# Experts' first tile: output projection by blocks of w_out, late scores for heads 4 to 7, gathers released slot by slot

## The chip, the core and the metric

The kernel runs on one core of a Trainium2 chip. The metric is the device time of one execution in microseconds (us). One program does a whole decoder layer for 1024 new prompt tokens and 32 sample tokens (8 sequences of 4).

## What is computed

The layer is: RMS norm, one input projection, a Mamba-2 group and a differential-attention group side by side, an output projection, then a mixer of single-neuron experts (PEER), per-layer input embeddings and a final norm. The change lies where the output projection and the mixer start:

```
h = h + concat([y_ssm, y_diff]) @ w_out
m = rmsnorm(h, g_ffn)
h = h + peer(m, w_query, sub_keys, expert_u, expert_v)

def peer(xn, ...):                      # blocks of 128 tokens
    q = (xt @ w_query).reshape(blk, 8, 2, 128)
    s = einsum('thcd,cnd->thcn', q, sub_keys)
    s1, i1 = top_k(s[:, :, 0], 16);  s2, i2 = top_k(s[:, :, 1], 16)
    sc, pos = top_k(s1[..., :, None] + s2[..., None, :], 16)
    idx = i1[pos // 16] * 128 + i2[pos % 16]
    act = gelu(einsum('thkd,td->thk', expert_u[idx], xt))
    return einsum('thk,thkd->td', softmax(sc) * act, expert_v[idx])
```

Every token reads 8 heads x 16 experts = 128 rows of `expert_uv`, each 2048 float32 (8 KB).

## The kernel before, in words

The program has three stages: `project`, `attend` and `experts`. All of the change is in `experts`. Each stage is written by hand for each engine: one program for SyncE (SP), GpSimd (POOL), ScalarE (ACT), VectorE (DVE) and TensorE (PE), which meet only at semaphores. What an engine's program has earlier is done earlier, whatever is ready.

`experts` works in tiles of 128 tokens: tiles 0 to 7 are the prompt, tile 8 the sample tokens. For a tile, POOL issues 128 indirect DMAs (`ring`, line 2526), the gathers; each brings one 8 KB row of `expert_uv` for each of the 128 partitions (1.05 MB) into one of the `RING = 8` slots. The first half of a slot's row is u, the second half v. A tile is cut in four groups of 32 tokens (`rows`, the copies of the normed activations to all quarters), so that one gather serves 32 tokens with four experts each.

For each gather c, DVE multiplies u by `rows` and sums (L2644). For each pair of gathers q, ACT makes the coefficients (`gelu`, times gate, into a diagonal: L2573, L2576, L2582) and PE adds coefficient times v into `acc` (L2704: eight instructions, the V sum of the pair). The V sum raises `v_used`, and POOL waits for `v_used` before it issues the gather that takes the same slot again (gather c needs the V sum of pair (c - 8) / 2).

Between the steps of these loops every engine takes `next()` steps of generators ("sides"): the front of the next tile, and in tile 0 also what is left of the tile's own search (`rest_vector`, `rest_scalar`) and the scores of the sample rows (`few_tensor`, L1983). So a side's order among the gathers is fixed.

Tile 0's front has nothing to hide behind. `front_tensor(pe, 0)` does, in this order:

- turns the mix `m` (L1738); ACT and DVE copy it to `aT` (L1799, L1833); DVE first waits for `g_in`, the load of g_ffn
- waits for all eight blocks of `wo` (w_out, one DMA per block of 128 rows, issued by ACT at L2535), then projects into `pt[0]` and `pt[1]` (L1753): first the eight blocks for the left half, then the eight for the right
- projects the sample rows (`few_project`, L1956)
- folds `w_queryT` with the keys into `w2` (`fold_queries`, L2100), chunk by chunk, 16 chunks. The chunks are loaded into the `ring` memory by SP, in four DMAs (L2482) behind a wait for all of `wo`. Banks `pk[2]`, `pk[3]` and `acc` hold the folds; ACT and DVE copy them out (L2544, L2548, L2112)
- turns the normed `m`, scores n = 0 (heads 0 and 1) behind chunk 3, folds the other chunks, copies the rows (`copy_rows`, L2138), and scores n = 1, 2, 3 (L1783, `pk[n]`)

Only then do the loop's seed of `acc` with h1 (L2687) and the first V sum follow. In the meantime DVE searches heads 0 and 1 (`search`) and writes their indices (`first_found`, L2024, semaphore `idx0`). POOL's program begins with `fold_out(pool, 15)`, the wait for ACT's copy of the last fold, since the first gathers overwrite the memory in which w_queryT lies; then it waits for `idx0`. Slot c of the ring holds chunks 2c and 2c + 1.

Of the kernel before, what the change touches and what calls it, by code (L numbers as in the profile page):

```python
# [14 lines left out]
P = 128  # L15
D = 1024
KT = D // P
# [25 lines left out]
PH, TOPK = 8, 16  # L43
# [1547 lines left out]
def experts(nc, t):  # L1591
# [18 lines left out]
    with ExitStack() as ctx:  # L1610
        st = Stage(nc, ctx, "ex")
        wo = st.sb("wo", [P, KT, D])
        w2 = st.sb("w2", [P, KT, 2 * PH * KEYS])
# [4 lines left out]
        aT = st.sb("aT", [P, KT, P])  # L1618
# [37 lines left out]
        acc = [st.ps(f"acc{k}", [P, 512]) for k in range(2)]  # L1656
        pt = [st.ps(f"pt{k}", [P, 512]) for k in range(2)]
        pk = [st.ps(f"pk{k}", [P, 4, KEYS]) for k in range(4)]
        consts, ident_in, g_in, keys_in, wo_in = (st.sem(n) for n in ("consts", "ident_in", "g_in", "keys_in", "wo_in"))
        idx0, negated0, grown0, divided0, gates0 = (  # L1660
            st.sem(n) for n in ("idx0", "negated0", "grown0", "divided0", "gates0"))
        wq_in = [st.sem(f"wq_in{n}") for n in range(4)]
        iota_up, set_up, folded = (st.sem(n) for n in ("iota_up", "set_up", "folded"))
# [71 lines left out]
        def front_tensor(pe, k):  # L1735
            def turn():
                for c in range(KT):
                    mm = pe.transpose(pt[c // 4][:, (c % 4) * P:(c % 4 + 1) * P], m[:, c * P:(c + 1) * P], ident[:])  # L1738
                mm.then_inc(turned, 1)

            yield from pause(4)
            pe.wait_ge(x_in, 32 * (k + 1))
            turn()
            if k == 0:
                few_turn(pe, 0)
            yield from pause(8)
            pe.wait_ge(taken_a, 2 * k + 1)
            pe.wait_ge(taken_v, 2 * k + 1)
            if k == 0:
                pe.wait_ge(wo_in, 16 * KT)  # L1750
            for n in range(2):
                for c in range(KT):
                    mm = pe.matmul(pt[n][:], aT[:, c, :], wo[:, c, n * 512:(n + 1) * 512],  # L1753
                                   start=(c == 0), stop=(c == KT - 1))
                    if c == KT - 1:
                        mm.then_inc(projected, 1)
                    if c % 3:
                        yield
            if k == 0:
                few_project(pe)  # L1760
                fold_queries(pe, 0, 4)
            yield from pause(18)
            pe.wait_ge(m_ready, k + 1)
            turn()
            if k == 0:
                fold_out(pe, 3)
                few_turn(pe, 1)
            yield from pause(8)
            pe.wait_ge(taken_a, 2 * k + 2)
            pe.wait_ge(taken_v, 2 * k + 2)  # L1770
            if k == 0:
                fold_out(pe, 2)
            if k == 1:
                pe.wait_ge(ranked, PAIRS)
                pe.wait_ge(few_ranked, 1)
            for n in range(4):
                if k == 0 and n == 1:
                    fold_queries(pe, 4, 2 * PH)
                    fold_out(pe, 2 * PH - 2)
                    fold_out(pe, 2 * PH - 1)  # L1780
                    copy_rows(pe, 0, range(GRP))
                for c in range(KT):
                    mm = pe.matmul(pk[n][:].rearrange("p j n -> p (j n)"), aT[:, c, :], w2[:, c, n * 512:(n + 1) * 512],  # L1783
                                   start=(c == 0), stop=(c == KT - 1))
                    if c == KT - 1:
                        mm.then_inc(scored, 1)
                    if c % 3:
                        yield
            if k == 0:
                return  # L1790
            yield from pause(48)
            pe.wait_ge(ranked, PAIRS * (k + 1))
            copy_rows(pe, k, (0, 1))
            yield

        def front_scalar(act, k):
            def take(n):
# [282 lines left out]
        def fold_out(eng, c):  # L2080

            if c in (1, 3):
                eng.wait_ge(fold_taken[1], c // 2 + 1)
            else:
                eng.wait_ge(fold_taken[0], c // 2 + 1 if c < 4 else c - 1)
# [384 lines left out]
        with nc.Block() as block:  # L2470
            @block.sync
            def _(sp):
# [3 lines left out]
                sp.dma_start(g[:], spread(t["g_ffn"])).then_inc(g_in, 16)  # L2476
                for c in range(2):
                    sp.dma_start(keysT[:, c, :], t["keysT"][:, c, :]).then_inc(keys_in, 16)
                sp.wait_ge(wo_in, 16 * KT)
                for n in range(4):  # L2480
                    src = t["w_queryT"][4 * n * P:4 * (n + 1) * P, :].rearrange("(c p) d -> p c d", p=P)
                    sp.dma_start(wqT[:, 4 * n:4 * n + 4, :], src).then_inc(wq_in[n], 16)  # L2482
# [28 lines left out]
            @block.gpsimd  # L2511
            def _(pool):
                pool.iota(iota_i, pattern=[[1, TOPK]], base=0, channel_multiplier=0).then_inc(iota_up, 1)
                fold_out(pool, 2 * PH - 1)
                for k in range(TILES):
                    if k < LAST:
                        pool.wait_ge(idx_ready, GRP * GRP * k)
                    else:
                        pool.wait_ge(few_idx, 1)
                    for i in range(TILE_CALLS[k]):  # L2520
                        c = FIRST_CALL[k] + i
                        if k == 0 and i % QUADS == 0:
                            pool.wait_ge(idx0, GRP * GRP * (i // QUADS + 1))
                        if c >= RING:
                            pool.wait_ge(v_used, (c - RING) // PAIR + 1)
                        pool.indirect_dma_start(ring[:, c % RING, :], None, t["expert_uv"],  # L2526
                                                bass.IndirectOffsetOnAxis(
                                                    (idx_cur[k % 2] if k < LAST else idx_few)[:, i:i + 1], 0)).then_inc(
                            came[c % RING], 16)

            @block.scalar
            def _(act):
                act.dma_start(ident[:], t["ident"]).then_inc(ident_in, 16)
                for k in range(KT):
                    act.dma_start(wo[:, k, :], t["w_out"][k * P:(k + 1) * P, :]).then_inc(wo_in, 16)  # L2535
                act.wait_ge(set_up, 2)
                first = front_scalar(act, 0)
                for _ in range(9):
# [127 lines left out]
            def _(pe):  # L2666
# [3 lines left out]
                for k in range(TILES):  # L2670
# [9 lines left out]
                    if k == LAST:  # L2680
                        for j in range(GRP):
                            mm = pe.matmul(acc[0][quarter(j), 0:BLK], ident[0:DEC, 0:DEC], h1[0:DEC, j * BLK:(j + 1) * BLK],
                                           start=True, stop=False, tile_position=(0, j * SUB))
                    else:
                        for n in range(2):
                            for first, at in placed(k, n):
                                mm = pe.matmul(acc[n][at, :], ident[:, first:first + at.stop - at.start],  # L2687
                                               h1[:, n * 512:(n + 1) * 512], start=True, stop=False,
                                               tile_position=(0, at.start))
                    mm.then_inc(seeded, 1)  # L2690
                    for q in range(FIRST_PAIR[k], FIRST_PAIR[k + 1]):
                        pe.wait_ge(diag_ready, q + 1)
                        last = FIRST_PAIR[k + 1] - q
                        for p in range(PAIR):
                            c = q * PAIR + p
# [6 lines left out]
                            for n in range(2):  # L2702
                                j = column_group((c - FIRST_CALL[k]) % GRP, n)
                                mm = pe.matmul(acc[n][quarter(j), :], diag[:, q % HALVES, p, :],  # L2704
                                               ring[:, c % RING, D + n * 512:D + (n + 1) * 512], start=False,
                                               stop=last <= 2, tile_position=(0, j * SUB))
                        mm.then_inc(v_used, 1)
                        for _ in range(PAIR):
                            for side in sides:
                                next(side, None)  # L2710
# [114 lines left out]
```

## Time and profile before

| | |
|---|---|
| median of 3 runs | 3608.3 us (3604.05 to 3608.34) |
| profiled execution, span from the first to the last instruction | 3606.9 us |
| mean granted clock of TensorE | 0.726 |
| PE busy | 2236.7 us, 62% |
| DVE busy | 2216.6 us, 61% |
| ACT busy | 1178.5 us, 33% |
| POOL busy | 1268.5 us, 35% |
| DMA moved | 1260.05 MB, mean 349 GB/s |
| start of the experts' stage in the span | about 766 us |

The span holds everything that the trace shows; the median is 1.4 us above it. Matmuls of float32 are two instructions each. Granted clock 0.50 is TensorE's lower level, 1.2 GHz, and 1.00 the higher one, 2.4 GHz. In a table by stretches the DMA share is that of the core's 16 DMA engines; 1.01 means that they are never free.

### The profile page before, as it was taken

To read this page: it belongs to the slowest core of one execution; us is meant where nothing else is said; L and a number is where in the kernel's file an instruction comes from. 1 tells how busy PE (TensorE), PEld (TensorE's weight loads), DVE (VectorE), ACT (ScalarE), POOL (GpSimd) and SP (SyncE) were. 2 spreads that over 40 slices of the span, in tenths; PEclk is the share of its full clock that TensorE was granted. 3 is DMA by queue.
4 is the path that set the end of the run, shared out by engine and by line. 5 is a ranking of instruction groups with operands and counts; after the bars stand their busy time and mean duration, and the time that the engine had idled before them with its cause. 6 is when DMAs were issued, how large, how long until landed. Compare 5 with 4: busy or idle time off the path is not lost.

```text
span 3606.9 us, 33674 instructions
## 1 busy us (share of the span) xinstructions
PE 2236.7 (62%) x9892; PEld 765.4 (21%) x9892; DVE 2216.6 (61%) x5337; ACT 1178.5 (33%) x3713; POOL 1268.5 (35%) x1243
## 2 busy tenths in 40 slices
PE   8999967868564554456355545634563654457775
PEld 3556533434110110011011101100110110012222
DVE  5325344626988558656855875586578557855555
ACT  2122214413423322422242242224223321354444
POOL 0000013202544444444444444444444443444342
PEclk9899978989675765567566757756675766577787
DMA  2211148875999999999999999999999999999997
GB/s 101 72 51 62 54 141 320 319 265 214 411 421 421 421 421 419 411 422 420 410 411 421 414 416 416 422 415 407 421 420 413 414 419 416 407 402 415 404 416 327
DMA packets 216450, 1260.05 MB, mean 349 GB/s; under 512 B 28677, under 2 KB 31450, under 8 KB 80882
## 3 DMA queue, kind: packets, MB, share of 16 engines
q0 software_dynamic: 165008, 1147.82, 77.6%
q1 hardware_dynamic: 46106, 101.76, 7.9%
q10 hardware_dynamic: 5152, 8.32, 0.7%
q8 instruction: 78, 1.28, 0.1%
q14 instruction: 106, 0.87, 0.1%
HBM read 1238.27 MB, written 24.05 MB: 350 GB/s over the span
## 4 chain that ended last, share of the span: by engine, by line
DMA 39%; PE 15%; DVE 8%; issue 7%; ACT 6%; POOL 3%; ACTq 0%; POOLq 0%; DVEq 0%; SPq 0%
DMA ex_ring<-in_expert_uv,ex_idx_cur 37%; PE ex_acc L2704 6%; PE ex_pk L2270 4%; POOL ex_ring L2526 3%; DVE ex_ring L2644 3%; PE ex_pk L1783 2%; ACT ex_diag L2582 2%; ACT ex_coef L2576 2%; DMA ex_ring<-in_expert_uv,ex_idx_few 1%; DVE ex_work L1927 1%; PE ex_pk L2138 1%; ACT ex_act_out L2573 1%; PE ex_pt L1753 1%; DVE ex_work L1920 1%; DVE ex_side_f L1932 1%
## 5 line engine op out<-in xcount | busy, mean ns | idle before, releaser
L2644 DVE CUSTOM_DVE_ANT_0 ex_ring<-ex_ring,ex_rows 128x1024 f32<-128x1024 f32 x1056 | 1291.1, 1224 | 849.6 <-DMA ex_ring<-in_expert_uv,ex_idx_cur 814.9
L2526 POOL DMA_INDIRECT ex_ring<-in_expert_uv,ex_idx_cur x1024 | 1136.1, 1109 | 1593.0 <-PE ex_acc L2704 1351.9
L2704 PE MATMUL ex_acc<-ex_ring,ex_diag 128*32 128x512 f32 x4096 | 828.0, 896 | 1107.8 <-ACT ex_diag L2582 1107.5
L2573 ACT ACTIVATE ex_act_out<-ex_dots 128x2 f32<-128x2 f32 x528 | 107.3, 203 | 1703.7 <-DVE ex_dots L2644 1703.1
L2704 PEld LDWEIGHTS ex_acc<-ex_ring,ex_diag 128*32 128x32 f32 x4096 | 97.0, 128 | 1771.5 <-ACT ex_diag L2582 1721.4
L2582 ACT ACTIVATE ex_diag<-ex_pick_row,ex_coef 128x32 f32<-128x32 f32 x1056 | 282.0, 314 | 50.5 <-ACT ex_coef L2576 1.5
L1783 PE MATMUL ex_pk<-ex_w,ex_aT 128*128 128x512 f32 x512 | 253.1, 637 | 0.0
L2576 ACT ACTIVATE ex_coef<-ex_act_out,ex_gate_cur 128x1 f32<-128x1 f32 x1024 | 245.6, 287 | 16.8
L340 PE MATMUL pj_bank<-pj_aT,pj_wbuf 128*128 128x512 f32 x512 | 226.7, 598 | 5.1 <-DVE pj_aT L529 5.1
L2270 PE MATMUL ex_pk<-ex_w,ex_aT 128*128 128x512 f32 x256 | 136.6, 680 | 26.4 <-issue 26.4
L1753 PE MATMUL ex_pt<-ex_wo,ex_aT 128*128 128x512 f32 x256 | 128.9, 647 | 9.1 <-DMA ex_wo<-in_w_out 9.1
L1783 PEld LDWEIGHTS ex_pk<-ex_w,ex_aT 128*128 128x128 f32 x512 | 96.9, 201 | 162.0 <-issue 161.9
L340 PEld LDWEIGHTS pj_bank<-pj_aT,pj_wbuf 128*128 128x128 f32 x512 | 96.3, 191 | 122.3 <-issue 117.7
L344 PE MATMUL pj_bank<-pj_wbuf,pj_aT 128*128 128x512 f32 x256 | 115.5, 606 | 0.0
L2644 DVE DVE_READ_ACCUMULATOR2_ANT ex_dots<- 128x1 f32 x1056 | 86.6, 82 | 0.0
L1423 ACT ACTIVATE at_s<-at_s,at_mn 128x128 f32<-128x128 f32 (+7 forms) x64 | 49.1, 768 | 98.6 <-DVE at_mn L1322 93.9
L2270 PEld LDWEIGHTS ex_pk<-ex_w,ex_aT 128*128 128x128 f32 x256 | 52.0, 215 | 116.0 <-issue 116.0
L1753 PEld LDWEIGHTS ex_pt<-ex_wo,ex_aT 128*128 128x128 f32 x256 | 49.5, 206 | 93.7 <-issue 93.7
L2138 PE MATMUL ex_pk<-ex_m,ex_ident 128*32 128x512 f32 x448 | 67.7, 758 | 2.7 <-ACT ex_rows L2161 2.7
L2573 ACT ACT_TABLE_LOAD x50 | 64.2, 1283 | 5.7 <-DVE ex_dots L2644 4.9
L1218 POOL DMA_DIRECT2D at_ring<-in_cache_v x64 | 35.0, 547 | 87.4 <-issue 78.3
L1218 POOL DMA_DIRECT2D at_ring<-in_cache_kT x64 | 35.0, 546 | 84.9 <-issue 84.9
(422 smaller groups left out, 2495.6 us busy)
## 6 DMA issues: line engine op xcount, KB each, us to landing
at_ring<-in_cache_kT SPq DMA_DIRECT2D x64, 256.0 KB, 9.4
at_ring<-in_cache_kT POOLq DMA_DIRECT2D x64, 256.0 KB, 6.0
at_ring<-in_cache_v SPq DMA_DIRECT2D x64, 256.0 KB, 8.9
at_ring<-in_cache_v POOLq DMA_DIRECT2D x64, 256.0 KB, 6.2
ex_ring<-in_expert_uv,ex_idx_cur POOLq DMA_INDIRECT x1024, 13.4
pj_wbuf<-in_w_in SPq DMA_DIRECT2D x6, 2048.0 KB, 10.5
ex_ring<-in_w_queryT SPq DMA_DIRECT2D x4, 2048.0 KB, 15.5
pj_aT<-in_xT_all SPq DMA_DIRECT2D x4, 1024.0 KB, 11.9
```

Source lines behind the costliest of these rows:

```text
L340: mm = pe.matmul(out[:], w[:, k, i * P:(i + 1) * P], aT[:, k, half * 512:(half + 1) * 512], start=(k == 0), stop=(k == KT - 1))
L344: mm = pe.matmul(out[:], aT[:, k, tile(i)], w[:, k, :], start=(k == 0), stop=(k == KT - 1))
L1753: mm = pe.matmul(pt[n][:], aT[:, c, :], wo[:, c, n * 512:(n + 1) * 512], start=(c == 0), stop=(c == KT - 1))
L1783: mm = pe.matmul(pk[n][:].rearrange("p j n -> p (j n)"), aT[:, c, :], w2[:, c, n * 512:(n + 1) * 512], start=(c == 0), stop=(c == KT - 1))
L2138: mm = pe.matmul(bank[quarter(q), :], ident[:, quarter(j)], m[:, n * 512:(n + 1) * 512], start=True, stop=True, tile_position=(0, q * SUB))
L2270: mm = pe.matmul(pk[half][0:n].rearrange("p j n -> p (j n)"), aT[:, c, 0:n], wg[:, c, half * 512:(half + 1) * 512], start=(c == 0), stop=( ...
L2526: pool.indirect_dma_start(ring[:, c % RING, :], None, t["expert_uv"], bass.IndirectOffsetOnAxis((idx_cur[k % 2] if k < LAST else idx_few)[ ...
L2573: act.activation(act_out[:, half, :], dots[:, half, :], ACT.Gelu).then_inc(gelu_done, 1)
L2576: act.activation(coef[:, half, p:p + 1], act_out[:, half, p:p + 1], ACT.Copy, scale=(gate_cur[k % 2] if k < LAST else gate_few)[:, i + p:i ...
L2582: ins = act.activation(diag[:, half, p, :], pick_row[:], ACT.Copy, scale=coef[:, half, p:p + 1])
L2644: dve.tensor_tensor_reduce(out=u, in0=u, in1=rows[:, j, :], scale=1.0, scalar=0.0, op0=ALU.mult, op1=ALU.add, accum_out=dots[:, q % HALVES ...
L2704: mm = pe.matmul(acc[n][quarter(j), :], diag[:, q % HALVES, p, :], ring[:, c % RING, D + n * 512:D + (n + 1) * 512], start=False, stop=las ...
```

## The change

- The one semaphore for w_out becomes one for each block. For tile 0 PE waits block by block, and multiplies both halves with a block before it goes to the next. The other tiles keep their order.
- SP waits for the sixth block (`wo_in[5]`) instead of all eight before it loads w_queryT.
- In tile 0, `front_tensor` scores n = 0 and 1 only. The scores of n = 2 and 3 (`score_late`) follow behind the V sums of pairs 0 and 1, ahead of the side steps.
- POOL's wait for ACT's copy of the last fold is gone. Instead each of the first eight gathers waits until PE has folded the two chunks that lie in its slot.

```diff
-        consts, ident_in, g_in, keys_in, wo_in = (...)
+        consts, ident_in, g_in, keys_in = (...)
+        wo_in = [st.sem(f"wo_in{c}") for c in range(KT)]
...
             if k == 0:
-                pe.wait_ge(wo_in, 16 * KT)
-            for n in range(2):
+                for c in range(KT):
+                    pe.wait_ge(wo_in[c], 16)
+                    for n in range(2):
+                        mm = pe.matmul(pt[n][:], aT[:, c, :], wo[:, c, n * 512:(n + 1) * 512],
+                                       start=(c == 0), stop=(c == KT - 1))
+                        if c == KT - 1:
+                            mm.then_inc(projected, 1)
+            for n in range(2 if k else 0):
...
-            for n in range(4):
+            for n in range(4 if k else 2):
                 if k == 0 and n == 1:
                     fold_queries(pe, 4, 2 * PH)
...
+        def score_late(pe, n):
+            for c in range(KT):
+                mm = pe.matmul(pk[n][:].rearrange("p j n -> p (j n)"), aT[:, c, :], w2[:, c, n * 512:(n + 1) * 512],
+                               start=(c == 0), stop=(c == KT - 1))
+            mm.then_inc(scored, 1)
...
-                sp.wait_ge(wo_in, 16 * KT)
+                sp.wait_ge(wo_in[5], 16)
...
-                fold_out(pool, 2 * PH - 1)
...
                         if c >= RING:
                             pool.wait_ge(v_used, (c - RING) // PAIR + 1)
+                        else:
+                            pool.wait_ge(folded, 2 * (c + 1))
...
-                    act.dma_start(wo[:, k, :], t["w_out"][k * P:(k + 1) * P, :]).then_inc(wo_in, 16)
+                    act.dma_start(wo[:, k, :], t["w_out"][k * P:(k + 1) * P, :]).then_inc(wo_in[k], 16)
...
                         mm.then_inc(v_used, 1)
+                        if q < 2:
+                            score_late(pe, 2 + q)
                         for _ in range(PAIR):
```

## Rows read from the trace of the kernel before

**Rows 1.** The page: its span, and the chain that ended last, by engine.
```profile
span 3606.9 us, 33674 instructions
...
DMA 39%; PE 15%; DVE 8%; issue 7%; ACT 6%; POOL 3%; ACTq 0%; POOLq 0%; DVEq 0%; SPq 0%
```

**Rows 2.** Stretches: us, then busy us of PE, PEld, DVE, ACT, POOL, clock, DMA.
```profile
786.00:788.00 2.00, 2.00 (x4) 0.76 (x3) 0.00 (x0) 0.00 (x0) 0.00 (x0) 0.50 0.70 184
788.00:791.00 3.00, 3.00 (x9) 1.32 (x8) 0.00 (x0) 0.00 (x0) 0.00 (x0) 1.00 1.03 422
...
860.00:875.00 15.00, 15.00 (x47) 6.02 (x49) 14.86 (x57) 5.62 (x19) 0.00 (x0) 1.00 0.58 242
...
920.00:940.00 20.00, 7.43 (x30) 1.32 (x28) 19.37 (x68) 8.60 (x29) 9.34 (x8) 0.70 1.01 421
...
2400.00:2700.00 300.00, 160.17 (x654) 35.58 (x654) 197.52 (x462) 93.96 (x345) 128.60 (x117) 0.65 1.01 417
```

**Rows 3.** The chain that ended last, 755 to 1100 us: start, us, what.
```profile
770.68 14.39 DMA ex_wo<-in_w_out
785.21 15.37 PE ex_pt L1753 x32
...
851.28 20.80 PE ex_pk L1783 x48
...
873.94 1.04 PE ex_acc L2704 x8
```

**Rows 4.** The trace in order of time, 750 to 900 us: start, us, engine, line.
```profile
777.47 0.69 DVE L1833 COPY ex_aT<-ex_pt 128x512 f32<-128x512 f32 x1 [10.71 <-DMA ex_g<-in_g_ffn]
...
786.20 0.33 PEld L1753 LDWEIGHTS ex_pt<-ex_wo,ex_aT 128*128 128x128 f32 x1 [0.52 <-issue]
787.05 0.33 PEld L1753 LDWEIGHTS ex_pt<-ex_wo,ex_aT 128*128 128x128 f32 x1 [0.52 <-issue]
```

**Rows 5.** Issue to landing: w_out (eight), first w_queryT, gathers 0, 8, 12.
```profile
DMA to landing us min/median/max: 7.1/11.8/14.4
...
DMA to landing us min/median/max: 8.5/8.5/8.5
...
DMA to landing us min/median/max: 5.7/5.7/5.7
...
DMA to landing us min/median/max: 7.0/7.0/7.0
...
DMA to landing us min/median/max: 12.1/12.1/12.1
```

**Rows 6.** The same trace for POOL: gathers 0, 8 and 12 being issued.
```profile
844.38 1.00 POOL L2526 DMA_INDIRECT ex_ring<-in_expert_uv,ex_idx_cur  x1 [77.83 <-ACT ex_w L2548]
...
875.24 0.94 POOL L2526 DMA_INDIRECT ex_ring<-in_expert_uv,ex_idx_cur  x1 [21.15 <-PE ex_acc L2704]
...
880.39 0.94 POOL L2526 DMA_INDIRECT ex_ring<-in_expert_uv,ex_idx_cur  x1 [0.39 <-PE ex_acc L2704]
```

**Rows 7.** The same for DVE and ACT: indices, u0, u1, u12; diagonals of V0, V2.
```profile
836.84 3.12 DVE L2024 CAST ex_idx_cur<-ex_idx_f 32x8 int32<-32x8 f32 x16
...
851.95 1.23 DVE L2644 CUSTOM_DVE_ANT_0 ex_ring<-ex_ring,ex_rows 128x1024 f32<-128x1024 f32 x1
...
859.19 1.21 DVE L2644 CUSTOM_DVE_ANT_0 ex_ring<-ex_ring,ex_rows 128x1024 f32<-128x1024 f32 x1
...
893.65 1.23 DVE L2644 CUSTOM_DVE_ANT_0 ex_ring<-ex_ring,ex_rows 128x1024 f32<-128x1024 f32 x1
...
862.55 0.53 ACT L2582 ACTIVATE ex_diag<-ex_pick_row,ex_coef 128x32 f32<-128x32 f32 x2
...
870.52 0.53 ACT L2582 ACTIVATE ex_diag<-ex_pick_row,ex_coef 128x32 f32<-128x32 f32 x2
```

**Rows 8.** The same for PE: steps of the sample's scores, and V5.
```profile
874.76 1.90 PE L1983 MATMUL ex_pk<-ex_w,ex_few_T 128*32 128x512 f32 x16
...
893.52 1.93 PE L2704 MATMUL ex_acc<-ex_ring,ex_diag 128*32 128x512 f32 x8 [4.64 <-ACT ex_diag L2582]
```

More of the change, by code:

```diff
@@ L1658, in experts @@
         pk = [st.ps(f"pk{k}", [P, 4, KEYS]) for k in range(4)]
-        consts, ident_in, g_in, keys_in, wo_in = (st.sem(n) for n in ("consts", "ident_in", "g_in", "keys_in", "wo_in"))
+        consts, ident_in, g_in, keys_in = (st.sem(n) for n in ("consts", "ident_in", "g_in", "keys_in"))
+        wo_in = [st.sem(f"wo_in{c}") for c in range(KT)]
         idx0, negated0, grown0, divided0, gates0 = (
```

## Prediction

> **What bounds the kernel now.** I read the page first: its own span, and the shares of the chain that ended last. DMA carries 39% of that chain, PE 15%, DVE 8% [rows 1]. The table by stretches then says when DMA is the limit. From 900 us on its engines are never free: share 1.01 at 421 GB/s in 920 to 940 us, and still 1.01 at 417 GB/s in 2400 to 2700 us [rows 2]. From there every gather waits for the 16 engines, and only an earlier arrival of the whole stream can shorten the run. So the question is what happens before: DMA share is only 0.58 in 860 to 875 us [rows 2]. The chain over the start of the experts' stage shows what it waits for [rows 3]: 14.39 us for the last block of w_out, 15.37 us of output projection, later 20.80 us for the scores of n = 1 to 3, then the first V sums, and only behind these the ninth gather. The trace in order of time (DVE, ACT, POOL, PE) gives the times at which each of these could have started.
>
> I number gathers from 0, u8 is VectorE's product with gather 8, V0 is the V sum of pair 0 (gathers 0 and 1). Eight ring slots: gathers 8 and 9 need V0, gathers 12 and 13 need V2.
>
> **Part 1, the projection by blocks.** Before, PE waits for all eight blocks, until 785.2 us. The blocks are issued one by one from 766.8 us and take 7.1 us (the first) to 14.4 us (the last) to land [rows 5], so the first is there at 773.9 and the last at 785.1, about 1.6 us apart. The projection needs aT too; its second half is copied by DVE at 777.47 + 0.69 = 778.16, late because DVE waits for g_ffn [rows 4]. So PE can start at 778.2, 7.0 us earlier. The same 32 instructions follow in another order (both halves of a block), with as many weight loads. Each takes 0.85 us at the low clock (787.05 less 786.20 [rows 4]) and 20.80 / 48 = 0.433 us at the full one [rows 3]. A block is four of them, 1.7 us at full clock and 3.4 us at the low one, and a block lands every 1.6 us or faster, with two already there at 778.2. PE therefore runs behind the landings and never waits: it comes to the last block at about 791.8, 6.7 us after that landed. The end is 778.2 + 15.37 = 793.6 where it was 800.6. **Gain 7.0 us.** DVE's additions to h1 still end one add behind the last matmul: the first half now comes 0.43 x 2 = 0.87 us before the end, longer than its add of 0.69.
> What isn't known is how long the clock stays at its low level. Before, it was 0.50 of full in 786 to 788 us and 1.00 from 788 [rows 2], some 3.2 us from the start. I take the same. Without any low stretch the 32 take 13.9 us (gain 8.5); with twice as long a one, 1.7 us more than 15.4 (gain 5.3). The Trainium skill ("TensorE: Matmul & The Clock Gate", section "What's actually happening") says that the moment at which the clock changes varies between runs of one kernel, since the monitor doesn't start with the kernel; the row shows one case only, and both ends above cover it.
> The rest of the front (projection of the sample rows, folds, norm, first scores, search of heads 0 and 1) is a chain of PE, ACT and DVE work with no transfer in it, and moves by 7.0 us as a whole.
>
> **Part 2, the load of w_queryT behind block 5.** SP issues it when the sixth block has landed, about 2.6 us (two blocks at 1.3) before 785.1. The first quarter landed 8.5 us behind its issue [rows 5], so at 793.6, and now near 791; the folds that need it start 3.5 us behind the projection, before at 804.1, now at 797.1. It is hidden either way; if the wait for all eight had stayed, 793.6 would still have done. Behind this wait on SP stand the four quarters, the constant pick_row and the two parking stores; all come no later. What the load can cost: it shares the engines with blocks 6 and 7. Even if both come 1.3 us later (one block's time), the last is there at 786.4, and is wanted at 791.8. I take 0.
>
> **Part 3, the gathers and their slots.** The first gather is released by ACT's last fold copy, at 844.38 [rows 6]. The other condition, its indices, was met when DVE's 16 copies ended at 836.84 + 3.12 = 839.96 [rows 7]. Now the indices alone count for the first ones: 839.96 - 7.0, and 0.3 to issue, 833.2, 11.2 us earlier; the wait for the folds of slot 7 (the last fold, near 836) is over before POOL, at 1.25 us a gather, comes to it at 842. What does it bring? u0 began at 851.95, directly behind DVE's copies of the rows, and u1 behind the search's first step, which waits for the scores of n = 1 [rows 7]; no early product waited for a landing. These move by 7.0 us with PE, and the gathers by at least 7.0 anyway. I take 0 from this part alone; it only makes the engines free earlier for gather 8. No engine waits more for it.
>
> **Part 4, the scores of n = 2 and 3 behind V0 and V1.** The coefficients of V0 were ready at 862.55 + 0.53 = 863.1 [rows 7], but PE was in the scores until 872.1 and seeded acc for 1.9 us; V0 ran at 873.94 for 1.04 us [rows 3]. Now:
> - n = 1 ends at 851.28 - 7.0 + 16 x 0.433 = 851.2, seeding at 853.1. The coefficients come at 863.1 - 7.0 = 856.1. V0 is 856.1 to 857.1, 17.8 us earlier.
> - Then 16 score instructions, 6.9 us, and two steps of the sample's scores (16 instructions, 1.7 us of the 1.90 shown, which overlaps at both ends [rows 8]), then V1: 857.1 + 6.9 + 1.7 + 1.0 = 866.8, where it ended at 877.5. 10.7 us earlier.
> - The same again: V2 ends at 876.5. Its coefficients (870.52 + 0.53 - 7.0 = 864.1 [rows 7]) don't hold it. Before, gather 12, which V2 releases, was issued at 880.39 [rows 6]; now at 876.8, **3.6 us earlier only**. Each late score holds up the V sums behind it.
> - But the gather lands sooner than that. Before, 8 to 11 had been issued within 5 us and 12 landed 12.1 us after its issue, at 892.5 [rows 5]. Now 8 to 11 are issued at 857.4 to 868.3 and are gone by 876. Gather 8 from idle engines took 7.0 us from its issue at 875.24 [rows 5, 6], so 12 lands at 876.8 + 7.0 = 883.8, **8.7 us earlier**. The very first gather took 5.7 us [rows 5]; that is the better end, 10.0 us.
> - DVE's side: the copy of aT for tile 1 waits for PE's turn behind V2, near 877.5; u11 is at 879.6 and u12, which began at 893.65 [rows 7], waits for its gather at 883.8, 9.8 us earlier. So DVE isn't the later one.
> The Trainium skill ("DMA: Bandwidth & Descriptors", section "Anatomy of one DMA — SWDGE (gpsimd) path") fits 2.0 us plus bytes at 436 GB/s, which is an estimate of 4.4 us for such a gather alone. No gather here landed that fast; by the page the lead would be 11.3 us. The trace decides.
>
> **The sum.** The stream of gathers stands 8.7 us earlier when the engines become full, 7.0 from the projection and 1.7 from the late scores (with the slots' release in it). Behind that a gather of 1.05 MB at 421 GB/s takes 2.5 us in both kernels, with as many bytes. DVE is busy 19.37 of 20 us in 920 to 940 [rows 2], so it is a second limit there, but its lead is no smaller. The profiled span is 3606.9 [rows 1] and becomes 3598.2; the median of the runs shown is 3608.3, 1.4 above the span, and becomes **3599.6 us**.
>
> **Rivals.**
> - A, forecast: lead 7 to 10 us, 3598 to 3601. Chance 0.52.
> - B, the clock falls before V0: PE now has nothing to do from 853.1 to 856.1, where it was in the scores before. For it: after 4.64 us without work eight V matmuls took 1.93 us [rows 8] instead of 1.04. Against: 3.0 us is shorter. Price: 3.4 us at low level loses 1.7 us, 7 us lose 3.4 us, all on V2 and gather 12; lead 7.0 to 5.3, and with a longer low stretch in the projection 3.6. That is 3601 to 3605. Chance 0.19.
> - C, more: no low stretch in the projection (8.5) and gather 12 within 5.7 us: 8.5 + 1.7 + 1.3 = 11.5 us, 3596.8. Chance 0.11.
> - D, the lead is given back: a stretch in which DVE or PE sets the pace regardless of when data come (DVE in 920 to 940 [rows 2]). It would have to lag by its own lead of 9.8; I see no work that doesn't move along. Were it so, 3606. Chance 0.10.
> - E, slower: the late scores run at low clock. Then each takes 16 x 0.85 = 13.7 us and the two sample steps 3.4, V sums 1.9: V2 ends at 856.1 + 1.9 + 2 x (13.7 + 3.4 + 1.9) = 896.0, gather 12 is issued at 896.3 and lands at 903.3, 10.8 us later than before: 3619. It turns from gain to loss once V2 ends later than about 885.2 (issue 0.3 later, and 885.5 + 7.0 = 892.5), which takes 2 x 8.7 = 17.4 us at the low level. Against it: the stretch has no idle time in which the clock could stay down. Chance 0.05.
> - F, slower: the projection by blocks runs at low clock throughout: 32 x 0.85 = 27.3 us, end 805.5, 4.9 us late; less 1.7, 3611.5. It decides from 2 x (8.5 + 1.7) = 20 us at the low level. The Trainium skill (the same TensorE page, "HAM oscillation — how this bites in real kernels") warns of just this form, short bursts with a wait for data in each. By that rule the time is this one; but blocks land faster than PE takes them, so no wait parts the bursts. Chance 0.03.
>
> **How the numbers follow.** Most likely A, 3599.6. The range takes in A, C, B and most of D: 3593 to 3607, which leaves out E, F and the worse end of D and of B, and some 7 us of what a run's median may differ. 0.2% (7.2 us, about what a measurement of this kernel can tell from no change) is 3601.1: faster holds most of A (0.43), C and a little of B, 0.56; same the rest of A, B and D, 0.36; slower E and F, 0.08.
>
> **What would show it.** Projection: its first matmul near 778 and its last near 793.6; a start at 785 says that a wait stayed. First gather near 833. V0 near 856, V1 near 866, V2 near 876, with 16 score matmuls between; granted clock 1.00 in 857 to 877 (B and E if not). Gather 12 landing near 884. DMA share 1.01 from about 879. If that start is 9 us earlier and the span isn't, D holds. The prediction is wrong if V2 ends later than 878, if gather 12 waits more than 7 us, or if the lead at 1100 us isn't the lead at the end.

## The result, and the profile after

| | before | after |
|---|---|---|
| median of 15 runs | 3608.06 us (3601.09 to 3612.4) | 3599.66 us (3596.14 to 3609.59) |
| ratio of the two | | 0.998, 95% interval 0.9973 to 0.9987 |
| profiled span | 3606.9 us | 3594.5 us |

At 3608 us the ratio is 7.2 us less (4.7 to 9.7). The forecast was 3599.6 us, a gain of 8.7. The two spans differ by 12.4 us, more than that, and 5.75 us of it lie ahead of the change. The first instruction of the experts' stage on POOL (its iota), first of before, then of after, in the traces in order of time:

```profile
766.41 0.14 POOL L2513 IOTA ex_idx_few<- 128x16 int32 x1 [24.21 <-POOLq L76]
```
```profile
760.66 0.14 POOL L2527 IOTA ex_idx_few<- 128x16 int32 x1 [24.74 <-POOLq L76]
```

`project` and `attend` are the same in both, yet this execution came to the stage 5.75 us earlier. In the profiles shown below the start lies anywhere from 761 to 774 us. So every time from here on that is called "from the start" is the trace's time less this row's. Counted like that, the stage took 3606.9 - 766.4 = 2840.5 us before and 2833.8 after: 6.7 us less, which fits the ratio.

The page of after; its chain is as before [rows 1], DMA first:

```profile
span 3594.5 us, 33674 instructions
...
DMA 40%; PE 15%; DVE 8%; issue 7%; ACT 6%; POOL 3%; ACTq 0%; SPq 0%; POOLq 0%; DVEq 0%
```

The changed stretch on PE, in order of time, with the two gathers that count (start, us, engine, line; in brackets the idle time before):

```profile
772.60 16.20 PE L1754 MATMUL ex_pt<-ex_wo,ex_aT 128*128 128x512 f32 x32 [2.21 <-issue]
...
851.35 1.16 PE L2719 MATMUL ex_acc<-ex_ring,ex_diag 128*32 128x512 f32 x8 [2.92 <-ACT ex_diag L2597]
852.44 8.69 PE L1806 MATMUL ex_pk<-ex_w,ex_aT 128*128 128x512 f32 x16
861.06 1.93 PE L1997 MATMUL ex_pk<-ex_w,ex_few_T 128*32 128x512 f32 x16
862.80 1.04 PE L2719 MATMUL ex_acc<-ex_ring,ex_diag 128*32 128x512 f32 x8
863.77 7.13 PE L1806 MATMUL ex_pk<-ex_w,ex_aT 128*128 128x512 f32 x16
870.84 1.92 PE L1997 MATMUL ex_pk<-ex_w,ex_few_T 128*32 128x512 f32 x16
872.58 1.04 PE L2719 MATMUL ex_acc<-ex_ring,ex_diag 128*32 128x512 f32 x8
```

The same trace for POOL, gathers 0, 8, 10 and 12 being issued (before in [rows 6]):

```profile
829.06 1.00 POOL L2541 DMA_INDIRECT ex_ring<-in_expert_uv,ex_idx_cur  x1 [68.26 <-DVE ex_idx_cur L2038]
...
852.79 0.94 POOL L2541 DMA_INDIRECT ex_ring<-in_expert_uv,ex_idx_cur  x1 [14.00 <-PE ex_acc L2719]
...
864.16 2.01 POOL L2541 DMA_INDIRECT ex_ring<-in_expert_uv,ex_idx_cur  x1 [9.19 <-PE ex_acc L2719]
...
873.92 0.94 POOL L2541 DMA_INDIRECT ex_ring<-in_expert_uv,ex_idx_cur  x1 [6.01 <-PE ex_acc L2719]
```

And three stretches of after (columns as in [rows 2]), with two of the long ones:

```profile
853.00:856.00 3.00, 3.00 (x5) 1.19 (x4) 2.96 (x16) 1.01 (x4) 1.67 (x2) 0.57 0.99 328
...
862.00:865.00 3.00, 3.00 (x23) 1.01 (x16) 2.90 (x11) 1.04 (x5) 0.84 (x1) 1.00 0.00 0
...
874.00:877.00 3.00, 3.00 (x30) 1.21 (x32) 2.25 (x4) 0.60 (x1) 1.80 (x2) 1.00 0.44 93
...
920.00:940.00 20.00, 6.84 (x32) 0.81 (x32) 19.81 (x74) 11.86 (x36) 10.44 (x8) 0.50 1.01 421
...
2400.00:2700.00 300.00, 158.20 (x654) 35.60 (x646) 198.25 (x461) 92.73 (x340) 129.24 (x118) 0.66 1.01 418
```

What is to be seen: the projection starts 11.9 us from the start instead of 18.8. V0 runs at 90.7 instead of 107.5. But PE is then busy without a gap and V2 ends only at 113.0 (113.7 before). The clock was at 0.57 just when the first late score ran. And the DMA engines stand idle twice, between the gathers 9 and 10 (share 0.00 in 862 to 865 us) and between 11 and 12 (0.44 in 874 to 877). From 877 us on they are full, at the same rate as before.

### The profile page after: what moved, and what is told of

The parts are those of the page before. It is cut to its first block, busy times and chain, and to the rows that moved or that the text cites. A ratio compares the mean times of both kernels' runs of the same rounds, so it can differ in the third digit from the quotient of the medians.

```text
span 3594.5 us, 33674 instructions
## 1 busy us (share of the span) xinstructions
PE 2226.4 (62%) x9892; PEld 762.3 (21%) x9892; DVE 2217.1 (62%) x5337; ACT 1178.6 (33%) x3713; POOL 1264.2 (35%) x1243
## 4 chain that ended last, share of the span: by engine, by line
DMA 40%; PE 15%; DVE 8%; issue 7%; ACT 6%; POOL 3%; ACTq 0%; SPq 0%; POOLq 0%; DVEq 0%
DMA ex_ring<-in_expert_uv,ex_idx_cur 38%; PE ex_acc L2719 6%; PE ex_pk L2284 3%; POOL ex_ring L2541 3%; DVE ex_ring L2659 3%; ACT ex_diag L2597 2%; ACT ex_coef L2591 2%; DMA ex_ring<-in_expert_uv,ex_idx_few 1%; PE ex_pk L1790 1%; PE ex_pk L2152 1%; ACT ex_act_out L2588 1%; DVE ex_work L1941 1%; DVE ex_work L1934 1%; DVE ex_side_f L1946 1%; PE ex_pt L1754 0%
## 5 line engine op out<-in xcount | busy, mean ns | idle before, releaser
L1790 PE MATMUL ex_pk<-ex_w,ex_aT 128*128 128x512 f32 x480 | 232.9, 625 | 0.0
L2284 PE MATMUL ex_pk<-ex_w,ex_aT 128*128 128x512 f32 x256 | 134.1, 670 | 25.5 <-issue 25.5
L1790 PEld LDWEIGHTS ex_pk<-ex_w,ex_aT 128*128 128x128 f32 x480 | 88.5, 197 | 150.0 <-issue 149.9
L1760 PE MATMUL ex_pt<-ex_wo,ex_aT 128*128 128x512 f32 x224 | 116.3, 661 | 0.0
L2284 PEld LDWEIGHTS ex_pk<-ex_w,ex_aT 128*128 128x128 f32 x256 | 51.1, 212 | 112.7 <-issue 112.7
L1322 DVE CUSTOM_DVE_ANT_0 at_s<-at_p_s,at_bias 128x128 f32<-128x128 f32 (+7 forms) x64 | 45.8, 753 | 28.0 <-PE at_p_s L1231 18.4
L1231 PE MATMUL at_p_s<-md_kT,md_qT 64*128 64x512 f32 (+3 forms) x192 | 43.6, 563 | 30.8 <-DVE at_mn L1322 20.7
```

Source lines behind the costliest of these rows:

```text
L2284: mm = pe.matmul(pk[half][0:n].rearrange("p j n -> p (j n)"), aT[:, c, 0:n], wg[:, c, half * 512:(half + 1) * 512], start=(c == 0), stop=( ...
```

## The experiments

Each kernel was timed in five rounds beside the kernel before; ratios are to that. The product of gather 20 (u20) is a good mark in the trace, since from there on the engines are full in every kernel.

### The projection by blocks alone

```diff
 # before.py, with wo_in[c] for each block, as in the change
             if k == 0:
-                pe.wait_ge(wo_in, 16 * KT)
-            for n in range(2):
+                for c in range(KT):
+                    pe.wait_ge(wo_in[c], 16)
+                    for n in range(2): ...
+            for n in range(2 if k else 0):
...
-                sp.wait_ge(wo_in, 16 * KT)
+                for c in range(KT):
+                    sp.wait_ge(wo_in[c], 16)
```

> The projection of tile 0 by blocks alone; SP still waits for all eight blocks, the late scores and the slot waits are left out. Theory 1 (the forecast's): the projection begins 7.0 us earlier and everything behind it moves along, so the V sum of pair 0, which was held by the scores of n = 1 to 3, moves by 7.0 us too, and the run by 6 to 7.5 us: about 3601 against 3608. Theory 2 (in the profile of the changed kernel the low clock lasted longer, projection 16.20 us instead of 15.37): 5.5 to 6 us, about 3602. Rival: the late scores carry the gain and this is under 3 us, 3605 or more.

Measured: 3603.72 us against 3608.46, ratio 0.9988 (0.9978 to 0.9998). In the trace the stage took 2834.4 us (2833.8 in the changed kernel) and u20 came at 140.1 from the start, where the changed kernel has 140.2. The landing that u20 waits for, in the chain of this kernel, whose stage started at 761.18:

```profile
889.83 11.42 DMA ex_ring<-in_expert_uv,ex_idx_cur
```

and in that of the changed kernel, started at 760.66:

```profile
887.82 13.02 DMA ex_ring<-in_expert_uv,ex_idx_cur
```

They end at 901.25 - 761.18 = 140.1 and 900.84 - 760.66 = 140.2. One part of the change gives the whole position of the stream. By the ratio it gives 4.3 us (0.7 to 7.9), less than the 6 to 7.5 of the first theory and than the 7.2 of the whole change, but the intervals overlap; that the rest of the change adds nothing is read from the traces and from the kernel without late scores below.

### The late scores alone

```diff
-            for n in range(4):
+            for n in range(4 if k else 2):
...
                         mm.then_inc(v_used, 1)
+                        if q < 2:
+                            score_late(pe, 2 + q)
```

> Only the scores of n = 2 and 3 move behind the V sums of pairs 0 and 1; projection, SP and the gathers' first wait are as before. Theory 1 (forecast): gather 12 issued 3.6 us earlier and landing 8.7 less 7.0 = 1.7 us earlier, run 1.7 us faster, 3606. Theory 2 (from the profile of the changed kernel, where V2 ended only 0.7 us earlier counted from the stage's start, the clock having fallen before V0): nothing or up to 2 us slower, gather 12 issued 1 us earlier to 1 us later than before less 7. Rival: freeing slots 0 and 1 some 10 us or more earlier fills the DMA engines and gives 4 us or more.

Measured: 3606.53 against 3608.46, ratio 0.9994 (0.9983 to 1.0005): no difference. Gather 12 was issued at 120.6 from the start (114.0 before), u20 came at 148.0 (146.0). The sample projection came 1.2 us later than in the profile of before, as the low clock had lasted longer in the projection; what is left, 0.8 us, is a loss. This kernel keeps the late release of the first gathers (gather 0 at 79.2): they landed until 106.5, and gather 8, issued at 99.3, only at 109.0. So it doesn't try the late scores as the forecast had them, with engines free for gather 8.

### The gathers' release alone

```diff
-                fold_out(pool, 2 * PH - 1)
...
+                        else:
+                            pool.wait_ge(folded, 2 * (c + 1))
```

> Only the release of the first eight gathers changes: by the folds of their slot's chunks instead of ACT's last fold copy. Theory 1 (forecast): first gather 4.1 us earlier than before (indices at 840.0 in the old profile's time, issue was 844.4), but no product waits for it and V0 stays behind the scores: 0, within 1 us of before. Rival: the early gathers matter because the DMA engines are the limit later: about 4 us faster.

Measured: 3608.78 against 3608.46, ratio 1.0 (0.999 to 1.0009). Counted from the sample projection, gather 0 was issued 3.6 us earlier than before and u20 came at 111.6 (111.9 before). Nothing waited for the first gathers.

### All but the late scores

```diff
-            for n in range(4 if k else 2):
+            for n in range(4):
...
-                        if q < 2:
-                            score_late(pe, 2 + q)
```

> The whole change without the late scores (all of n = 0 to 3 ahead of the loop, as before). Theory 1: V0 follows 7.0 us earlier than before, the run gains 7.0: 1.7 us slower than the changed kernel. Theory 2 (late scores bring nothing in time): equal to the changed kernel within 1 us, about 6 us faster than before. Rival: the late scores carry the gain, and this one is within 2 us of before.

Measured: 3600.78, ratio 0.9978 (0.9967 to 0.9989), u20 at 140.1, 111.5 behind the sample projection. That is the second theory: the late scores bring nothing in time.

### What PE time ahead of V1 and V2 costs

```diff
         def score_twice(pe, n):
+            for _ in range(2):
                 for c in range(KT): ...   # as score_late
```

> The changed kernel with each late score multiplied twice, 7 us more of PE work behind V0 and again behind V1 (results unchanged). Theory: V1 ends 7 us and V2 14 us later, gather 12 is issued near 127 us from the stage's start and lands near 134, and with the DMA engines idle in between the run is 12 to 14 us slower than the changed kernel, 4 to 6 us slower than before: the forecast's rival E by its cost. Rival: the DMA stream absorbs it, as it absorbed the late scores themselves: 7 us slower or less.

Measured: 3615.98 against 3607.91, ratio 1.0017 (1.0008 to 1.0026), so by the two ratios 13.3 us slower than the changed kernel. Its late scores and V sums on PE:

```profile
863.32 1.93 PE L2720 MATMUL ex_acc<-ex_ring,ex_diag 128*32 128x512 f32 x8 [2.93 <-ACT ex_diag L2598]
865.18 14.74 PE L1807 MATMUL ex_pk<-ex_w,ex_aT 128*128 128x512 f32 x32
...
881.59 1.04 PE L2720 MATMUL ex_acc<-ex_ring,ex_diag 128*32 128x512 f32 x8
882.56 14.00 PE L1807 MATMUL ex_pk<-ex_w,ex_aT 128*128 128x512 f32 x32
...
898.24 1.04 PE L2720 MATMUL ex_acc<-ex_ring,ex_diag 128*32 128x512 f32 x8
```

V2 ends at 899.28 - 773.67 = 125.6 from the start (113.0), and u20 comes at 152.1 (140.2). 12.6 us of delay to V2 are 11.9 us at u20: from where the changed kernel stands, PE time ahead of V2 goes into the run almost in full.

### The late scores one V sum later

```diff
-                        if q < 2:
-                            score_late(pe, 2 + q)
+                        if q in (1, 2):
+                            score_late(pe, 1 + q)
```

> The changed kernel with the late scores one V sum later: n = 2 behind V1 and n = 3 behind V2 instead of V0 and V1. Theory (a late score costs the V sums behind it 7 to 9 us and so undoes what the early V0 gives): gathers 10 and 11 are issued near 95.5 us from the stage's start instead of 103.5, gather 12 near 105 instead of 113, u16 near 127 instead of 129.6, and the run is 2 to 3 us faster than the changed kernel. Rival (the engines' DMA stream starts where it starts, whatever PE does first): u20 stays 112 us behind the start of the sample projection and the run is as the changed one.

Measured: 3596.67 against 3607.91, ratio 0.9971 (0.9961 to 0.9982). Gather 10 at 96.8, 11 at 98.9, 12 at 106.6, u20 at 139.2, 1.0 us ahead of the changed kernel though its projection ended 0.4 us later. The interval overlaps that of the changed kernel; the trace shows the direction, less than the 2.6 us at u16 that I expected (129.0 against 129.6). The order isn't the only thing that differs: the clock fell here too (0.52 behind V0), but it was up again when the late scores ran, 7.13 us each. Kernels that kept the clock up part the two. There u20 comes 110.8 and 110.1 behind the sample projection with the late scores behind V0 and V1 (the next kernel, and the one with fillings before the projection), and 108.7 and 109.5 with them behind V1 and V2 (the last two kernels, which also have the wait for g_ffn moved).

### The clock before V0

PE stands idle for 2.9 us before V0, and in the changed kernel the clock fell there.

```diff
                     mm.then_inc(seeded, 1)
+                    if k == 0:
+                        fill(pe, pt[0], 3, 512)   # 12 products of ident with itself, 128 columns each
```

> The changed kernel with 12 small matmuls of the identity (into pt[0], not used) in the 2.9 us that PE stands idle before V0. Results are the same. Theory (the clock's fall before V0 costs the late scores 1.7 us): the score of n = 2 takes 7.0 us instead of 8.6, V1 and V2 end 1.7 us earlier (gather 12 near 111.5 us from the stage's start instead of 113.3), and what the late scores were to bring appears: u20 1 to 1.7 us earlier, 111 us behind the start of the sample projection instead of 112.1; the run up to 1.7 us faster than the changed kernel. Rival: the V sums come earlier but u20 stays at 112.

Measured: 3599.09 against 3606.49, ratio 0.9981 (0.9972 to 0.9989), as the changed kernel. In the trace the clock and the score are as the theory has them:

```profile
848.93 2.94 PE L1740 MATMUL ex_pt<-ex_ident 128*128 128x128 f32 x24
851.92 1.06 PE L2727 MATMUL ex_acc<-ex_ring,ex_diag 128*32 128x512 f32 x8
852.92 7.13 PE L1812 MATMUL ex_pk<-ex_w,ex_aT 128*128 128x512 f32 x16
```

The score takes 7.13 us instead of 8.69, gather 12 is issued at 111.8 (113.3) and u20 comes at 139.0 (140.2), 110.8 behind the sample projection instead of 112.1. That is a gain of 1.2 us in one profile, too small for the ratios. Gather 13 still landed at 121.5 (121.4 in the changed kernel), gather 17 at 131.6 (132.7). What lies between isn't shown; in that stretch the changed kernel's DMA engines moved one packet of instructions (0.02 MB, 128 to 130 from the start), which here came at 114 to 116, beside the gap.

The other kernels bear the clock's part out. Seven have PE idle for 2.92 or 2.93 us before V0. In six of them the clock fell (0.50 to 0.58 in the 3 us from 1.5 us behind V0's start, 0.69 with the scores twice), and a score right behind V0 took 8.64 to 8.83 us; in the seventh, the one with fillings before the projection, it stayed at 1.00. In the three kernels with this gap filled it stayed at 1.00.

### The start of the projection

```diff
 # DVE
-                dve.wait_ge(g_in, 16)              # head of the program
...
             dve.wait_ge(inverted, k + 1)
+            if k == 0:
+                dve.wait_ge(g_in, 16)              # where g is used
```

> The changed kernel, with DVE's wait for g_ffn moved from the head of its program to the multiplication with g. Theory (the forecast's, that the start of the projection is set by DVE's copy of aT behind g_ffn): the copy is made right behind PE's turn, the projection starts about 2 us earlier (at 9.7 to 10 us from the stage's start instead of 11.9), the sample projection behind it 2 us earlier too, at 26 to 26.7, and the run is 2 us faster than the changed kernel, 10 us faster than before. Rival: the blocks or the low clock set the pace from there, and it brings under 0.7 us.

Measured: 3602.4 against 3607.91, ratio 0.9981 (0.9971 to 0.9992). The projection starts at 10.0 from the start and takes as long as before, with all its blocks in time:

```profile
774.88 16.20 PE L1754 MATMUL ex_pt<-ex_wo,ex_aT 128*128 128x512 f32 x32
```

The sample projection is 1.9 us earlier, u20 1.7 us (138.5). At u64 1.3 of it are left, at u96 0.8, at u128 none (416.5, 416.2 in the changed kernel). What set the start was as forecast; the gain isn't seen in the run.

### Fillings before the projection

```diff
                 pe.wait_ge(ident_in, 16)
+                fill(pe, acc[1], 5, P)
...
                 few_turn(pe, 0)
+                fill(pe, acc[1], 4, P)
```

> The changed kernel with small matmuls of the identity (into acc[1], not used) ahead of the first turn and behind the sample rows' turn, so that PE works from the arrival of the identity to the start of the projection. Theory (the low clock costs the projection 1.4 to 3 us): the projection takes 13.9 to 14.5 us instead of 16.1, the sample projection starts at 26 us from the stage's start instead of 28.1 and the run is about 2 us faster than the changed kernel. Rival: with the clock up the blocks' landings set the pace and it gains under 0.7 us.

Measured: 3601.67 against 3606.49, ratio 0.9985 (0.9975 to 0.9994). It missed: the projection started at 13.1 instead of 11.9 and took 15.6 us, and the sample projection came at 28.7 (28.1). The fillings were not what held it. The second ended 10.7 from the start, and PE then waited for DVE's copy of aT, which stood behind the load of g_ffn for 1.1 us longer than in the changed kernel. The trace, whose stage starts at 765.53:

```profile
775.04 1.16 PE L1740 MATMUL ex_acc<-ex_ident 128*128 128x128 f32 x8
...
777.80 0.69 DVE L1854 COPY ex_aT<-ex_pt 128x512 f32<-128x512 f32 x1 [11.92 <-DMA ex_g<-in_g_ffn]
...
856.81 1.06 PE L2727 MATMUL ex_acc<-ex_ring,ex_diag 128*32 128x512 f32 x8 [2.92 <-ACT ex_diag L2604]
857.81 7.13 PE L1813 MATMUL ex_pk<-ex_w,ex_aT 128*128 128x512 f32 x16
```

And its stretches: the second filling, the idle time behind it, and the projection.

```profile
774.50:776.30 1.80, 1.70 (x16) 1.47 (x16) 0.00 (x0) 0.39 (x1) 0.00 (x0) 1.00 1.00 392
776.30:778.50 2.20, 0.00 (x0) 0.00 (x0) 0.69 (x1) 0.00 (x0) 0.00 (x0) 1.00 1.05 394
778.60:781.00 2.40, 2.40 (x5) 1.15 (x6) 0.00 (x0) 0.00 (x0) 0.00 (x0) 0.78 1.03 406
781.00:784.00 3.00, 3.00 (x6) 1.21 (x5) 0.00 (x0) 0.00 (x0) 0.00 (x0) 0.61 0.87 332
```

So the fillings had raised the clock, PE was without work for 2.39 us, and the clock fell again within the projection. Before V0 PE had the same 2.92 us without work as in the changed kernel, the clock stayed up, the score took 7.13 us, and u20 came at 138.8, 110.1 behind the sample projection.

### Together

The wait for g_ffn and the later late scores; then these with both fillings; then with the filling before V0 only.

> Both of these edits. If each is worth what the first theory says and they add up: 4 to 5 us faster than the changed kernel, 12 to 13 us faster than before, about 3595.5. If only the wait for g_ffn matters: 2 us faster than the changed kernel.

Measured: 3596.02 against 3607.91, ratio 0.9965 (0.9951 to 0.9978).

> All edits that pointed the right way: wait for g_ffn moved, late scores behind V1 and V2, both fillings. If the gains add up: 3 us from the later late scores, 2 from the fillings and 1 to 2 from g_ffn against the changed kernel, 3593 to 3595, ratio 0.996. If the blocks' landings or the tile's end swallow the lead: as the kernel with the later late scores and g_ffn alone, 0.9965.

Measured: 3594.8 against 3606.49, ratio 0.9968 (0.9958 to 0.9977), u20 at 135.3, u128 at 412.8.

> The changed kernel with the wait for g_ffn moved, the late scores behind V1 and V2 and the filling before V0 only; the filling before the projection, which in its own run ended 1.1 us behind the time at which the projection could have started, is left out. Theory: sample projection at 25.6 to 26.2 us from the stage's start, score of n = 2 at full clock, u20 near 135.5 us, and the run 11 to 13 us faster than before, ratio 0.9965 or a little under. Rival: a lead won in tile 0 beyond 7 us is given back by its end: u128 at 415 to 416 us as in the others and ratio 0.998 as for the changed kernel.

Measured: 3596.99 against 3608.73, ratio 0.9967 (0.9954 to 0.998), u20 at 135.7, u128 at 413.6. The reason given for leaving the filling out holds for the kernel before this one and not for the one that it names: with g_ffn out of the way the copy of aT was ready at 9.5 from the start there, but the projection started at 11.7, directly behind the second filling, where it starts at 9.7 without it.

The three agree: 0.9965 to 0.9968, some 12 us faster than before, and all three medians are below the changed kernel's. Which of the edits carries how much of the last 4 to 5 us isn't settled: the intervals overlap, and the leads in the trace shrink within tile 0, 4.9 us at u20 to 3.4 at u128 in the second of them.

## Why the prediction came out, and where it didn't

The marks of six profiles, each from its stage's start in us; worked out from the rows of the traces:

| | before | blocks only | late only | after | filling before V0 | late twice |
|---|---|---|---|---|---|---|
| projection starts | 18.8 | 12.2 | 18.6 | 11.9 | 11.9 | 11.7 |
| sample projection starts | 34.1 | 28.3 | 35.3 | 28.1 | 28.2 | 27.0 |
| V0 starts | 107.5 | 101.7 | 98.0 | 90.7 | 90.9 | 89.7 |
| gather 8 issued | 108.8 | 103.0 | 99.3 | 92.1 | 92.2 | 91.9 |
| gather 10 issued | 111.4 | 105.6 | 110.8 | 103.5 | 102.0 | 109.3 |
| gather 12 issued | 114.0 | 108.2 | 120.6 | 113.3 | 111.8 | 125.9 |
| u20 starts | 146.0 | 140.1 | 148.0 | 140.2 | 139.0 | 152.1 |
| u20 less sample projection | 111.9 | 111.8 | 112.7 | 112.1 | 110.8 | 125.1 |

**Right: the projection.** Its start was forecast 7.0 us earlier and is 6.9. Its length was taken as the 15.37 us of the profile of before; it is 16.1 here. But the same holds for the old order: with "late only" the sample projection comes 16.7 us behind the projection's start, with "gathers only" 16.5, and with "late twice", which has the blocks, 15.3. The difference is the low clock: its 0.85 us from one weight load to the next go on until 787.9 in the profile of before, 2.7 us from the projection's start, and until 777.0 in that of after, 4.4 us. The low clock lasts differently long from run to run, in both orders, as the Trainium skill says of it ("TensorE: Matmul & The Clock Gate", section "What's actually happening"; by that rule, the traces agree). So the profile of before was a short case, and the gain of this part is nearer to its 6.9 us at the start than to the 6.0 between the two profiles: the three kernels with the old order (before, "late only", "gathers only") average 35.0 at the sample projection, the changed kernel and "blocks only" 28.2, 6.8 us. Rival F didn't come: PE ran for 16.2 us without a gap, so there was no wait between bursts of the kind that the Trainium skill's section "HAM oscillation — how this bites in real kernels" (same page) is about.

**Right: the load of w_queryT and the gathers' release at nothing.** SP issued the load at 777.99 - 760.66 = 17.3 from the start instead of 18.7, 1.4 us and not 2.6 earlier, hidden either way. Gather 0 came 9.6 us earlier. The early release gave nothing alone (ratio 1.0), and nothing beside the blocks (u20 at 140.1 with it and without it). Whether the late scores need it wasn't tried by itself.

**Wrong: the late scores.** The step "V2 ends at 876.5", 110.1 from the start, came out at 113.0. 1.0 us of it is the longer projection (V0 began at 90.7, not at 89.7). Of the other 1.9 us, 1.6 are the clock: rival B, at its first size. From V0's start to V2's end it is 22.3 us here and 20.6 with the filling before V0; the rest is that a score takes 7.13 us at the full clock and not 6.9. The stretch 853 to 856 has clock 0.57, and the score of n = 2 took 8.69 us. With the filling it took 7.13 us, and V2 and u20 were earlier by 1.5 and 1.2 us.

The term of the sum was 1.7 us and measured nothing: u20 behind the sample projection is 111.9 before, 111.8 with blocks only, 111.5 without the late scores, 112.1 after. The account can be made from the issues alone. With blocks only, the engines are full from gather 8, issued at 103.0. After, gathers 8 and 9 were issued at 92.1, while the engines were at the last of gathers 0 to 7 (gather 7 landed at 95.5): two gathers ahead, 2 x 2.5 = 5.0 us. Gather 10 then comes at 103.5, 0.5 us later than gather 8 did there, and its pair is 5.0 us of work for the engines; but gathers 12 and 13 come 9.8 us after gather 10, so the engines miss 4.8 us. 5.0 - 0.5 - 4.8 is -0.3 us, against -0.1 measured at u20 (-0.3 counted from the sample projection). This is an estimate; the shares of the DMA engines agree with it, from 100 to 130 us from the start, blocks only first, then after:

```profile
861.18:891.18 30.00, 19.93 (x136) 5.37 (x135) 23.75 (x75) 8.90 (x29) 14.73 (x13) 0.82 0.89 361
```
```profile
860.66:890.66 30.00, 25.21 (x143) 8.65 (x142) 24.25 (x74) 9.95 (x32) 15.44 (x12) 0.89 0.70 273
```

That is 3.3 us idle against 9.0, 5.7 us more, where the account has 5.3. What V0 wins, V2 gives back. I had seen that each late score holds up the V sums behind it, and took the rest too high by 1.7 us. By the traces the clock decides most of it: in the two kernels with the late scores behind V0 and V1 in which it stayed up, u20 comes 110.8 and 110.1 behind the sample projection, 0.9 to 1.6 us sooner than the 111.7 that the four kernels without late scores average ("gathers only" is the fourth, 111.6); in the three in which it fell (after, "late only", and the kernel with the wait for g_ffn moved) 112.1 to 112.7.

The prediction's marker hides this. It took the landing of gather 12 for the lead of the whole stream. u12 did come 8.3 us earlier (127.2 and 119.0), 1.7 us of it not there with blocks only (120.7). But gather 13 landed at 121.7 with blocks only and at 121.4 after, and at u16 the two are level (129.8 and 129.6): one gather that lands early on idle engines is no lead of the stream. Of the signs that the prediction gave for being wrong, one came: V2 ends later than 878 in the time of before, 111.6 from the start. The second didn't: u12 began 5.7 us behind the issue of gather 12.

**Right: the stream carries the lead to the end.** 5.8 us at u20 (146.0 and 140.2), 5.8 at u256 (748.6 and 742.8), 6.7 for the whole stage; rival D didn't come for the changed kernel. It did, for one profile, with the wait for g_ffn alone: its extra 1.7 us were gone by u128. By which mechanism isn't known.

**Rival E as a price.** It asked 17.4 us at the low clock for the turn from gain to loss, 8.7 us of delay to V2. With the late scores multiplied twice V2 was 12.6 us late and the run 13.3 us slower, 0.0017 slower than before. At that price the turn lies where 7.2 us are lost, some 7 us of delay to V2; this is an estimate, as no kernel stands at the turn, and the low clock itself never lasted so long.

So 8.7 was 7.0 + 1.7, and is 6.8 + 0; the measured 7.2 (4.7 to 9.7) holds both sums, and only the single parts tell them apart. What ran is rival B with its lead of 7.0, and not A. That the median of 3599.66 stands at the 3599.6 of A is luck: the ratio alone, 7.2 us off the forecast's 3608.3, would give 3601.1.

## What to carry to other kernels

When a ring of buffers holds up a transfer stream, count how many transfers are out and when the next pair follows, not when the first slot is freed: a slot freed 17 us early was worth two transfers, and the work moved behind it opened a gap of the same size. By the traces here, work that must go somewhere costs less one release later: with the clock up, behind V1 and V2 instead of V0 and V1 gave 0.6 to 2.1 us more at u20. And compare profiles from a landmark just ahead of the change: single spans of this kernel differ by more than the change is worth, for reasons that lie in stages it doesn't touch.

## What the runs showed of the hardware

- The start of the experts' stage in the profiles of kernels with the same `project` and `attend` lay between 760.7 and 773.7 us. I had not expected single executions to differ so much ahead of the change.
- TensorE's low clock after an idle time of 2.92 us: granted 0.57 in the stretch from 1.7 to 4.7 us behind it, and a 16-instruction score 1.6 us longer than with the 2.9 us filled. It isn't so each time: it fell in six of the seven profiles with such an idle time before V0, and stayed at 1.00 in that of the kernel with fillings before the projection. There it fell after another idle time, of 2.39 us before the projection (1.00 in it, 0.61 in 781 to 784 us).
- In the kernels without fillings the projection of 32 instructions took from 15.3 to 16.9 us, counted from its start to the sample projection, with the same instructions: the low clock lasted 2.7 us from its start in one profile (before), 4.4 us in another (after).
